# A hybrid decoder layer on one core: the head's transfers and squares, the first weight sums and the vector engine's order rearranged

## The reference

```python
def rmsnorm(x, w):
    y = xf * lax.rsqrt(jnp.mean(xf * xf, axis=-1, keepdims=True) + EPS)
    return y * w
def swiglu(x, w_gate, w_up, w_down):
    return (jax.nn.silu(x @ w_gate) * (x @ w_up)) @ w_down
# the layer
x = x + 0.5 * swiglu(rmsnorm(x, ffn1_norm), gate1, up1, down1)
x = x + hybrid_mixer(rmsnorm(x, mix_norm), ...)
x = x + 0.5 * swiglu(rmsnorm(x, ffn2_norm), gate2, up2, down2)
y = rmsnorm(x, final_norm)
```

## Time and profile before

| | us |
|---|---|
| three timed runs | 1172.77, 1176.02, 1831.43 |
| median | 1176.02 |
| profiled execution | 1177.34 |
| its span | 1175.5 |
| TensorE matmul busy | 1137.8 (97%) |
| VectorE busy | 761.5 (65%) |
| ScalarE busy | 447.8 (38%) |
| Pool busy | 442.6 (38%) |

### The profile page before, as it was taken

The page is one execution under the profiler, slowest core; times in us unless marked ns, Lnnn a source line. Parts: engine busy times, 40 slices in busy tenths (PEclk is TensorE's granted clock), DMA queues, the critical chain, the costliest instruction groups (busy, mean ns, idle before and its releaser), DMA issues.

```text
span 1175.5 us, 20165 instructions
## 1 busy us (share of the span) xinstructions
PE 1137.8 (97%) x8532; PEld 993.8 (85%) x8532; DVE 761.5 (65%) x921; ACT 447.8 (38%) x600; POOL 442.6 (38%) x284
## 2 busy tenths in 40 slices
PE   7989999999999999999999899999899999999996
PEld 6889899988998887877887766888799899989985
DVE  3899368945877576543446277646997379836953
ACT  5444134522435434311224366434443144424431
POOL 0364068604833000313101188621571278316811
PEclk9999999999999999999999799999999999999997
DMA  6134323332332321123112001032233223423211
GB/s 223 36 96 159 108 72 108 107 108 87 95 105 90 108 76 68 37 73 109 37 53 51 8 2 37 2 107 72 72 108 108 90 91 108 131 84 108 80 65 71
DMA packets 33022, 98.45 MB, mean 84 GB/s; under 512 B 3376, under 2 KB 7984, under 8 KB 31280
## 3 DMA queue, kind: packets, MB, share of 16 engines
q1 hardware_dynamic: 32656, 97.10, 25.3%
q10 hardware_dynamic: 288, 0.24, 0.1%
HBM read 95.24 MB, written 2.10 MB: 83 GB/s over the span
## 4 chain that ended last, share of the span: by engine, by line
PE 89%; DVE 5%; issue 2%; ACT 2%; POOL 1%; DMA 0%; POOLq 0%; DVEq 0%; ACTq 0%
PE bank L574 24%; PE bank L575 23%; PE bank L576 23%; PE bank L1890 3%; PE bank L1657 2%; PE bank L1688 2%; PE bank L621 1%; PE bank L1673 1%; DVE hb_lo L690 1%; PE bank L1948 1%; PE bank L1937 1%; PE bank L1944 1%; PE bank L1942 1%; PE bank L1496 1%; PE bank L1316 0%
## 5 line engine op out<-in xcount | busy, mean ns | idle before, releaser
L574 PE MATMUL bank<-hb_hi,w_hi 128*128 128x256 f32 x1064 | 299.8, 282 | 8.4 <-DVE w_lo L917 8.4
L575 PE MATMUL bank<-hb_lo,w_hi 128*128 128x256 f32 x1064 | 299.6, 282 | 0.0
L576 PE MATMUL bank<-hb_hi,w_lo 128*128 128x256 f32 x1064 | 299.6, 282 | 0.0
L574 PEld LDWEIGHTS bank<-hb_hi,w_hi 128*128 128x128 f32 x1064 | 202.0, 190 | 9.1 <-DVE w_lo L917 8.8
L575 PEld LDWEIGHTS bank<-hb_lo,w_hi 128*128 128x128 f32 x1064 | 201.9, 190 | 0.3
L576 PEld LDWEIGHTS bank<-hb_hi,w_lo 128*128 128x128 f32 x1064 | 202.0, 190 | 0.0
L898 POOL TENSOR_TENSOR w_sum<-raw 128x512 f32<-128x512 f32 x38 | 59.0, 1553 | 332.8 <-PE bank L576 332.8
L574 PE MATMUL bank<-act_hi,w_hi 128*128 128x512 f32 x448 | 179.9, 402 | 0.0
L575 PE MATMUL bank<-act_lo,w_hi 128*128 128x512 f32 x448 | 179.2, 400 | 0.0
L576 PE MATMUL bank<-act_hi,w_lo 128*128 128x512 f32 x448 | 179.2, 400 | 0.0
L862 ACT ACTIVATE w_hi<-raw 128x1536 fp32r<-128x1536 f32 (+1 forms) x67 | 108.6, 1621 | 169.0 <-PE bank L576 168.9
(11 more groups left out here) (281 smaller groups left out, 1745.3 us busy)
## 6 DMA issues: line engine op xcount, KB each, us to landing
raw<-in_gate_up SPq DMA_DIRECT2D x44, 1024.0 KB, 5.5
raw<-in_w_in SPq DMA_DIRECT2D x13, 1024.0 KB, 4.8
raw<-in_down SPq DMA_DIRECT2D x8, 1024.0 KB, 5.1
raw<-in_down SPq DMA_DIRECT2D x16, 512.0 KB, 4.1
raw<-in_down SPq DMA_DIRECT2D x8, 768.0 KB, 4.2
raw<-in_w SPq DMA_DIRECT2D x8, 512.0 KB, 3.9
x<-in_x SPq DMA_DIRECT2D x4, 512.0 KB, 6.6
raw<-in_w_out SPq DMA_DIRECT2D x4, 512.0 KB, 4.7
```

Of the source, the lines that this page charges most:

```text
L574: pe.matmul(out_ap, wh, xh, start=first, stop=False)
L575: pe.matmul(out_ap, wh, xl, start=False, stop=False)
L576: return pe.matmul(out_ap, wl, xh, start=False, stop=last)
```

## The change

- SP: the first step's weights go as two transfers of 512 KB, a half of the contraction each, in the order x 0, half 0, x 1, x 2, half 1, x 3. ScalarE issues only the norms' columns of the parameters at the start; the rest goes by SP at step 8.
- Squares of the head: ScalarE squares two tiles at a time into four buffers, VectorE adds the four and folds them, and TensorE sums the one tile that is left after step 0. The broadcast moves from step 0 into step 1. A root of one column on ScalarE stands ahead of the norm's.
- Pool makes the sums of step 3 with counts of their own (`s_early`): three of the four as soon as the weights have landed, in five operations in place of four, and the fourth (S[0]) when step 1 is done. Then it waits for the fifth `hb` low part before it sums step 4. In all steps S[3] comes ahead of S[2], and the vector split of the first half needs only three sums.
- VectorE and ScalarE: the order up to step 4 is rearranged, and step 4's splits move ahead of the end of the start functions. Step 2 is evacuated into `c_next` (the room of `h_raw`) in place of `c_sb`. In step 3 the second half of the sums is split first.
- The last Down step of the second layer signals its first bank singly.

```diff
-HB_LO_ORDER = (1, 3, 2, 0, 5, 4, 6)
+HB_LO_ORDER = (1, 0, 3, 2, 5, 4, 6)
...
+        def act_head_square(act, c):
+            act.wait_ge(x_landed[c], 16)
+            act.activation(SQ_HEAD[c], x[:, 2 * c:2 * c + 2, :], ACT.Square).then_inc(head_sq, 1)
+
+        def dve_head_sum(dve, c):
+            dve.wait_ge(head_sq, c + 1)
+            if c > 1:
+                dve.wait_ge(head_sum, c - 1)
+            dve.tensor_tensor(sq, sq, SQ_HEAD[c], ALU.add).then_inc(head_sum, 1)
+
+        def dve_head_fold(dve):
+            dve.wait_ge(head_sum, 3)
+            dve.tensor_tensor(sq_sum[:, :], sq[:, 0, :], sq[:, 1, :], ALU.add).then_inc(head_sum, 1)
...
         def act_ffn_start(act, f):
 
             st = FFN[f]
-            act_split_ffn(act, st[1])
+            if f:
+                act_split_ffn(act, st[1])
             act_rms(act, 2 * f)
-            act_r(act, 2 * f)
+            if f:
+                act_r(act, 2 * f)
+                act_split_ffn(act, st[2])
+            else:
+                act_split_ffn(act, st[2])
+                act_r(act, 2 * f)
             act_hb(act, f, 1)
-            act_split_ffn(act, st[2])
             act_hb(act, f, 0)
             act_hb(act, f, 2)
+            act_split_ffn(act, st[3])
             act_hb(act, f, 3)
             act_evac(act, st[0])
+            act_split_sum(act, st[3], 1)
             act_hb(act, f, 5)
             act_hb(act, f, 4)
-            act_split_ffn(act, st[3])
             act_hb(act, f, 6)
-            act_split_sums(act, st[3])
+            act_split_sum(act, st[3], 0)
+            act_split_ffn(act, st[4])
+            act_split_sums(act, st[4])
             act.wait_ge(step_done, splits(st[2].step) + 1)
             act_evac(act, st[1])
 
         def dve_ffn_start(dve, f):
 
             st = FFN[f]
-            dve_split_ffn(dve, st[1])
+            if f:
+                dve_split_ffn(dve, st[1])
             dve_rstd(dve, 2 * f)
+            if f == 0:
+                dve_split_ffn(dve, st[2])
             dve_hr(dve, f, K_HIGH, KT // 2)
             dve_hr(dve, f, K_LOW, 0)
+            if f:
+                dve_split_ffn(dve, st[2])
             dve_hb(dve, f, 1)
-            dve_plain(dve, st[0])
-            dve_split_ffn(dve, st[2])
+            dve_plain_evac(dve, st[0], c_sb)
             dve_hb_sum(dve, f, 3)
             dve_hb_sum(dve, f, 5)
             dve_hb_sum(dve, f, 4)
             dve_hb_sum(dve, f, 6)
+            dve_plain_evac(dve, st[1], c_sb)
+            dve_split_ffn(dve, st[3])
+            dve_hb(dve, f, 0)
             dve_hb(dve, f, 3)
+            dve_split_sums(dve, st[3], 1)
+            dve_split_sums(dve, st[3], 0)
             dve_hb(dve, f, 2)
-            dve_hb(dve, f, 0)
-            dve_plain_evac(dve, st[1])
-            dve_split_ffn(dve, st[3])
             dve_hb(dve, f, 5)
-            dve_split_sums(dve, st[3], 0)
-            dve_gated(dve, st[1])
             dve_hb(dve, f, 4)
             dve_hb(dve, f, 6)
-            dve_split_sums(dve, st[3], 1)
+            dve_plain_evac(dve, st[2], c_next)
+            dve_split_ffn(dve, st[4])
+            dve_split_sums(dve, st[4], 0)
+            dve_gated(dve, st[1])
+            dve_split_sums(dve, st[4], 1)
             dve_act_lo(dve, st[1])
...
+                    if f == 0 and start and t == 1 and k == KT - 1:
+                        pe_head_sum(pe)
+                    if f == 0 and st is FFN[0][1] and (t, k) == (0, 1):
+                        pe_norm_bc(pe, m)
...
+                    if st is FFN[1][-1] and ab == 0:
+                        mm.then_inc(last_half, 1)
...
+        def pool_first_sums(pool, st):
...
+            pool.wait_ge(raw_landed[par], 16 * (st.step // 2 + 1))
+            pool.tensor_tensor(S[1], A[3], A[2], ALU.add).then_inc(s_early, 1)
+            pool.tensor_tensor(S[2], A[1], A[3], ALU.subtract).then_inc(s_early, 1)
+            pool.wait_ge(s_early, 4 * st.f + 1)
+            pool.tensor_tensor(S[1], S[1], A[1], ALU.subtract).then_inc(s_early, 1)
+            pool.wait_ge(s_early, 4 * st.f + 3)
+            pool.tensor_tensor(S[3], A[0], S[1], ALU.subtract).then_inc(s_early, 1)
+            pool.wait_ge(step_done, splits(st.step) - 1)
+            pool.wait_ge(s_early, 4 * st.f + 4)
+            pool.tensor_tensor(S[0], A[3], A[2], ALU.add).then_inc(s_sum, 4)
...
         def pool_ffn(pool, f):
-            for st in FFN[f][PLAIN:]:
+            pool_first_sums(pool, FFN[f][PLAIN])
+            pool.wait_ge(hb_lo_dve, 7 * f + 5)
+            for st in FFN[f][PLAIN + 1:]:
                 if summed(st):
                     pool_weight_sums(pool, st)
...
+        def sp_head(sp):
+            sp_x(sp, 0)
+            sp_first(sp, 0)
+            sp_x(sp, 1)
+            sp_x(sp, 2)
+            sp_first(sp, 1)
+            sp_x(sp, 3)
...
-            for k in range(KT):
-                if k == HEAD_SUMS:
-                    act_split_first(act)
-                act_square(act, 0, k)
-                act_hp(act, 0, k)
+            act_hp(act, 0, 0)
+            act_hp(act, 0, 1)
+            act_split_first(act, 0)
+            act_hp(act, 0, 2)
+            act_hp(act, 0, 3)
+            act_head_square(act, 0)
+            act_head_square(act, 1)
+            act_hp(act, 0, 4)
+            act_hp(act, 0, 5)
+            act_split_first(act, 1)
+            act_head_square(act, 2)
+            act_hp(act, 0, 6)
+            act_hp(act, 0, 7)
+            act_head_square(act, 3)
+            act_split_ffn(act, FFN[0][1])
+            act.wait_ge(eps_set, 1)
+            act.activation(root_first, eps_col, ACT.Sqrt)
...
+            dve_hp(dve, 0, 0)
+            dve_hp(dve, 0, 1)
+            dve_split_first(dve, 0)
+            dve_hp(dve, 0, 2)
+            dve_hp(dve, 0, 3)
+            dve_hp(dve, 0, 4)
+            dve_hp(dve, 0, 5)
+            dve_head_sum(dve, 1)
+            dve_split_first(dve, 1)
+            dve_hp(dve, 0, 6)
+            dve_hp(dve, 0, 7)
+            dve_head_sum(dve, 2)
+            dve_head_sum(dve, 3)
+            dve_head_fold(dve)
+            dve_split_ffn(dve, FFN[0][1])
```

More of the change, by code:

```diff
@@ L900, in pool_weight_sums, with half_order, act_split_sum @@
             pool.tensor_tensor(S[1], S[0], A[1], ALU.subtract).then_inc(s_sum, 1)
-            pool.tensor_tensor(S[2], A[1], A[3], ALU.subtract).then_inc(s_sum, 1)
             pool.wait_ge(s_sum, 4 * st.s + 2)
             pool.tensor_tensor(S[3], A[0], S[1], ALU.subtract).then_inc(s_sum, 1)
+            pool.tensor_tensor(S[2], A[1], A[3], ALU.subtract).then_inc(s_sum, 1)
+        def pool_first_sums(pool, st):
+            par = st.step % 2
+            A = [raw[:, par, b * BLOCK:(b + 1) * BLOCK] for b in range(4)]
+            S = [w_sum[:, par, (3 + b) * BLOCK:(4 + b) * BLOCK] for b in range(4)]
+            pool.wait_ge(raw_landed[par], 16 * (st.step // 2 + 1))
[8 more added lines that the diff above has]
+            pool.tensor_tensor(S[0], A[3], A[2], ALU.add).then_inc(s_sum, 4)
+        def half_order(st):
+            return (1, 0) if st is FFN[st.f][PLAIN] else (0, 1)
+        def act_split_sum(act, st, half):
+            c = sum_cols(half)
+            if st is FFN[st.f][PLAIN] and half:
+                act.wait_ge(s_early, 4 * st.f + 4)
+            else:
+                act.wait_ge(s_sum, 4 * st.s + 2 * (half + 1))
+            act.activation(w_hi[:, st.step % 2, c], w_sum[:, st.step % 2, c], ACT.Copy).then_inc(s_hi, 1)
         def act_split_sums(act, st):
-            par = st.step % 2
             for half in range(2):
-                c = sum_cols(half)
-                act.wait_ge(s_sum, 4 * st.s + 2 * (half + 1))
-                act.activation(w_hi[:, par, c], w_sum[:, par, c], ACT.Copy).then_inc(s_hi, 1)
+                act_split_sum(act, st, half)
         def dve_split_sums(dve, st, half):
@@ L914, in dve_split_sums @@
             c = sum_cols(half)
-            dve.wait_ge(s_hi, 2 * st.s + half + 1)
-            dve.wait_ge(s_sum, 4 * st.s + 4)
+            dve.wait_ge(s_hi, 2 * st.s + half_order(st).index(half) + 1)
+            if st is FFN[st.f][PLAIN] and half:
+                dve.wait_ge(s_early, 4 * st.f + 4)
+            else:
+                dve.wait_ge(s_sum, 4 * st.s + 3 + half)
             dve.tensor_tensor(w_lo[:, par, c], w_sum[:, par, c], w_hi[:, par, c].bitcast(F32),
@@ L927, in act_evac @@
                 act.wait_ge(post_done, 5 * st.n + 5)
-                act.activation(gate_sb, c_sb, ACT.Silu).then_inc(silu_ready, 1)
+                if st is FFN[st.f][PLAIN - 1]:
+                    act.wait_ge(act_raw_ready, st.n // 2)
+                act.activation(gate_sb, c_next if st is FFN[st.f][PLAIN - 1] else c_sb, ACT.Silu).then_inc(silu_ready, 1)
             else:
@@ L940, in act_ffn @@
             for before, st, then in after(f)[PLAIN:]:
-                if then:
+                if then is FFN[f][PLAIN + 1]:
+                    pass
+                elif then:
```

(27 more changed lines are left out.)

86 lines of the change are left out of this document (42 added, 44 removed).

## The result

The changed kernel took 1153.64 us (median of four runs, 1150.44 to 1162.30) beside 1174.58 for the kernel before: a ratio of 0.9846, 95% interval 0.9813 to 0.9880. (One of the four executions behind 1174.58 took 1831.43 us; it counts as a slow one, and the ratio leaves it out.) That is 1.5% faster, inside the 2% band; forecast were 1161 and a range of 1152 to 1169. The number came out. Its terms did not, as the experiments show: half of the measured gain or more is in none of them.

What follows compares the result with a forecast made beforehand. TensorE was taken as the bound nearly everywhere, so only its waits and low clock could pay. 12.8 + 3.3 + 3.4 - 4.0 = 15.5 us off 1177.34 gave 1161.8 (1160.5 against the median); forecast 1161, range 1152 to 1169.

Steps and rivals of the forecast that it cites:

- The head: Kernel start: first real matmul at 9.4 us, nine us sooner; clock up after 4 to 6 us; h products from 28.4.
- the term of 12.8: First FFN: VectorE's full queue ends step 5's split at 72.7, so step 5 starts there instead of 85.5, gaining 12.8 us.
- The six collisions: First FFN: VectorE operations slowed beside Pool's sums of steps 4 and 5, about 1.1 us each, 6 us in all.
- the starting point, 85.5: First FFN: time in us at which step 5 began before the change, from which the gain was counted.
- Second FFN, 3.3 less 2.0: Second FFN: step 5 starts at 863.7 instead of 867.0, gain 3.3 us, less 2.0 for slow clock after its new wait.
- Slow clock, 4.0: Both FFNs: TensorE runs at 1.2 GHz after each new wait for step 5's split, costing 2.0 us each, 4.0 together.
- Tail, 3.4: End of the kernel: tile 6 is handled while TensorE works, so the last broadcast comes 3.0 to 3.9 us sooner, taken 3.4.
- Counted at nothing, root_first: Head: the root's table load is done ahead and was hidden already before, so it is worth nothing.
- (a): Rival, both FFNs: VectorE keeps up and TensorE is the bound throughout, gain 28.7 us, time 1148; chance 0.12.
- (b): Rival, head gives less: clock rises only 12.5 us after the start, or weight halves land late; 1166 us; chance 0.22.
- (d): Rival, head: halves land no sooner than 14, TensorE starts at 16.5, first FFN gives 5.8; 1169 us; chance 0.06.
- (c): Rival, both FFNs: Pool and VectorE collide at every two-input operation, slower than before, 1180 us; chance 0.04.

Runs made afterwards that it cites:

- b1: Kernel before plus one unused one-column tile, which moves the streamed operands 32 bytes on, no instruction changed: 1162.39 us, ratio 0.9906.
- t1: Kernel before with only the last Down step's first bank signalled singly (the tail alone): 1170.08 us, ratio 0.9954.
- a1: The changed kernel run again, unedited: 1152.38 us, ratio 0.9838.
- a2: Changed kernel with hb 3 and the first Silu ahead of step 3's split on ScalarE, and step 3's gate product behind step 5's split on VectorE: 1147.98 us.
- b2: Changed kernel with root_first put into eps_col's tile, so streamed operands keep the addresses of the kernel before: 1168.08 us, ratio 0.9965.
- t4: Changed kernel with Pool's weight sums of steps 4, 5 and 6 replaced by zeros in both layers (output not the layer's): 1139.96 us, one run.
- t3: Kernel before with only the new Pool, VectorE and ScalarE order, old head and old tail: 1180.98 us, ratio 1.0055.
- a4: Changed kernel with all four x transfers issued ahead of both halves of the first weights: 1164.52 us, one run.
- t2: Kernel before with only the new head, root_first included, old order behind the h products and old tail: 1157.56 us, ratio 0.9853.
- a3: Changed kernel with Pool's five early sums (step 3) waiting for the end of step 1: 1152.18 us, one run.
- b3: a2 plus an unused 32-byte tile that moves the weights to 0 modulo 64, streamed operands staying at 32: 1160.07 us, ratio 0.9894.
- b4: b3 with root_first in eps_col's tile too, so weights and streamed operands are both at 0 modulo 64: 1144.71 us, ratio 0.9760.

## Why the prediction was right, and where it was not

**The head: right.** First real matmul 9.98 (9.4), clock up six us later (4 to 6), h products from 29.2 (28.4), evacuation of step 1 at 42.63 (42.1).

**First FFN, the term of 12.8: too large.** Two steps of it failed. The queue from the evacuation of step 1 to the end of split 5 took 34.0 us, not 30.6. The six collisions were right; missing are the 2.6 us in which VectorE waits for a Pool sum that it had itself held up, and 0.8 of small gaps. The prediction had counted that wait at nothing: step 4's sums from 52, wanted at 59, and at most 1.1 us of one sum. Pool began at 52.47, but its three sums took 7.6 us, where three alone take 3.9, and VectorE was ready at 57.5. And the starting point, 85.5, is Pool's mark again (TensorE's step 5 began at 85.23) and belongs to one execution: before, r_sb came at 32.68 in the profile, in b1 and t1, which have the same head, at 30.24 and 30.38, since the clock had risen sooner (the spacing fell at 24.8, not 30.9). At the start of step 6, behind the new wait and its slow clock, the changed kernel leads by 95.08 - 88.44 = 6.6 us against that profile, and by 91.88 - 88.23 = 3.7 from b1 to a1. Forecast were 10.8 (12.8 less 2.0).

**Second FFN, 3.3 less 2.0: wrong in sign.** Up to the evacuation of step 1 the sum was right: 20.4 us behind r_sb, forecast 20.3. Then the same 34.0 in place of 30.6 follow (825.04 to 859.03), so that step 5 gains nothing and loses 0.5 us. The slow clock behind its wait is then a net cost: step 6 starts 65.9 us behind r_sb, before 63.95, in b1 63.0. The layer lost 2 to 3 us; a2 shows that 3.0 were to be had back by order.

**Slow clock, 4.0: right.** From step 5 to step 6 the profile has 11.8 and 11.4 us, a step without a wait 9.9: 3.4 in all.

**Tail, 3.4: right**, 3.6.

**Counted at nothing, root_first: wrong.** The sentence on the root called its table load hidden already and worth nothing. That is so (before, it ended 4.1 us ahead of the sum that the root waits for); but its tile is worth 10 us (b1) to 15 us (b2 against the changed kernel), which no term of the sum holds.

**The sum.** By places in the profiles, scheduling gave 6.6 - 2.0 + 3.6 = 8.2 us of the 15.0 between the two profiled executions, and 3.7 - 2.9 + 3.6 = 4.4 from b1 to a1. By medians it is 4.1 with unequal addresses (b2) and 9 to 10 with equal ones (b1 to the changed kernel, measured apart; 5.0 of it are the clock in the mixer, below). 15.5 had been forecast for it. What filled the gap was the address effect. By medians it is 10 to 15 us; in the profiled pair, whose changed kernel had the slow value through its first FFN, it is less: of the 6.8 us that scheduling leaves, 5.3 lie behind the start of step 6 in the second layer (113.3 ns in place of 117.3), 0.6 behind that of the first, 0.9 in the mixer. The forecast held because two errors of like size stood against each other: its mechanism is right in kind, and that the number came out is luck.

**The rivals.** (a), TensorE the bound: would hold without Pool's sums (t4), not here; that the time nevertheless came near its 1148 goes with the spacing. (b) and (d) fell with the head. (c) did not happen at 1180, though t3 shows that the order without the new head is slower.

**Open.** Medians and places leave about 5 us between them in the equal-address pair, and the profiles put them in the mixer. From the first FFN's last matmul to the second layer's r_sb b1 takes 436.8 us and a1 431.8, and in it TensorE is at the lower clock level for 30.6 and for 20.4 us. Two stretches of b1's mixer:

```profile
569.00:573.00 4.00, 4.00 (x31) 0.64 0.00 0
641.00:647.00 6.00, 6.00 (x21) 0.50 0.00 0
```

In a1, which comes there some 5 us sooner:

```profile
564.00:568.00 4.00, 4.00 (x75) 1.00 0.00 0
635.00:641.00 6.00, 6.00 (x42) 1.00 0.01 3
```

All 14 profiles go together in this: with 30.6 us at the lower level (t1, b1) the mixer takes 436.8 us, with 27.2 (before, changed, a4) 435.0 to 435.9, with 23.8 (t3, t4) 433.4 to 433.9, with 20.4 (a1, b2) 431.8 to 431.9, with 10.2 to 13.6 (t2, a2, a3, b3, b4) 428.6 to 429.0. How much it is differs between executions of one kernel. The four profiles with the old head have 23.8 to 30.6 us of it, the ten with the new head 10.2 to 27.2; whether the head has a part in that is not shown. Nor was the head tried with the tail and the old order, which by the places would stand some 2 us ahead of the changed kernel; the best version run is b4, 1144.71 us, 0.7% below the changed kernel's repeat.

## What to carry to other kernels

Before a gain is put down to a schedule, compare the spacing of back-to-back matmuls in both traces, and where an edit adds or drops a tile, look at what it moved: one unused tile of 32 bytes was worth as much here as the rewritten head, tail and order together, or more. When two engines lock each other out, follow both queues: the delay of the engine that isn't the bound comes back through its semaphore. Take a starting point from more than one execution where the clock's rise is in it. And set the granted clock of the timed runs beside their times: here it hid some 5 of the 14 us that the unused tile is worth in the profiles.

## What the runs showed of the hardware that was not expected

The place of TensorE's two SBUF operands relative to each other, modulo 64 bytes, changes the spacing of 256-column fp32r matmuls at granted clock 1.00 between 113.3 and 117.3 to 118.7 ns, and the time of this kernel by 0.9% with no instruction changed. At equal places there are two levels, 113.3 and 117.8, of which one holds for tens of us and which differ between executions of one kernel: 4.5 ns x 84 matmuls are 0.4 us a step. Of the 9.3 us between the changed kernel's two traces 6 are this, and 3 are the time that TensorE spends at its lower clock level in the mixer, where 10 us more at that level cost 5. A Pool sum of 1.29 us beside an unbroken run of two-input vector operations took 3.34 us, and the run itself no longer than without Pool's sums (4.63 us for four, in t4 as well).
